# Experts sorted by load into places of 256 to 128 slots, in a two-layer hybrid diffusion step on one core

## The reference

```
def swiglu(h, w1, w3, w2):
    return (jax.nn.silu(h @ w1) * (h @ w3)) @ w2

def moe_swiglu(h, router, w1, w3, w2):
    probs = jax.nn.softmax((h @ router).astype(jnp.float32), axis=-1)
    top_p, top_i = lax.top_k(probs, TOP_K)
    top_p = top_p / jnp.sum(top_p, -1, keepdims=True)
    gates = jnp.sum(jax.nn.one_hot(top_i, N_EXPERTS, dtype=jnp.float32) * top_p[..., None], axis=-2)
    y = jnp.zeros(h.shape, jnp.float32)
    for e in range(N_EXPERTS):
        y = y + gates[..., e:e + 1] * swiglu(h, w1[e], w3[e], w2[e]).astype(jnp.float32)
    return y.astype(h.dtype)
```

## Time and profile before

| | |
|---|---|
| median of 3 runs | 2710.22 us (2710.1 to 2718.47) |
| the profiled execution | 2724.16 us, span 2722.3 us |
| mean granted TensorE clock | 0.975 |
| TensorE, VectorE, ScalarE busy | 93%, 51%, 41% |
| instructions | 68039 |

### The profile page before, as it was taken

The page is one execution under the profiler, slowest core; times in us unless marked ns, Lnnn a source line. Parts: engine busy times, 40 slices in busy tenths (PEclk is TensorE's granted clock), DMA queues, the critical chain, the costliest instruction groups (busy, mean ns, idle before and its releaser), DMA issues.

```text
span 2722.3 us, 68039 instructions
## 1 busy us (share of the span) xinstructions
PE 2521.7 (93%) x30324; PEld 2197.1 (81%) x30324; DVE 1401.3 (51%) x2474; ACT 1128.5 (41%) x2126; POOL 146.1 (5%) x163
## 2 busy tenths in 40 slices
PE   6998799898899999989987999998999999999996
PEld 3996577676798999969965777766899999999995
DVE  2337455556533333362374665474565555555565
ACT  3226544544421211242255545444444444444452
POOL 0002000010000000010010010001000000000011
PEclk8999899999999999999998999998999999999998
DMA  7223023320122222222200222202765666566672
GB/s 273 78 78 127 24 74 96 96 75 27 70 77 72 78 78 78 72 72 78 78 11 1 66 66 66 65 5 109 240 209 178 214 212 207 183 211 211 181 259 83
DMA packets 82701, 304.58 MB, mean 112 GB/s; under 512 B 9376, under 2 KB 9504, under 8 KB 82272
## 3 DMA queue, kind: packets, MB, share of 16 engines
q1 hardware_dynamic: 71072, 257.93, 29.6%
q0 software_dynamic: 11328, 42.21, 4.2%
HBM read 273.11 MB, written 27.00 MB: 110 GB/s over the span
## 4 chain that ended last, share of the span: by engine, by line
PE 83%; DVE 8%; issue 3%; ACT 3%; DMA 1%; POOL 0%; SPq 0%; another core or an unknown queue 0%; DVEq 0%; ACTq 0%; POOLq 0%
PE ps L451 19%; PE ps L452 19%; PE ps L453 19%; PE ps L1183 7%; PE ps L812 3%; PE ps L917 2%; PE ps L464 2%; PE ps L1115 2%; PE ps L960 1%; PE ps L976 1%; DMA ring<-in_blocks 1%; PE ps L463 1%; DVE arena L2474 1%; DVE arena L2473 1%; PE ps L1167 1%
## 5 line engine op out<-in xcount | busy, mean ns | idle before, releaser
L2278 DVE TENSOR_TENSOR ring_lo<-ring,w_ffn 128x1024 fp32r<-128x1024 f32 x264 | 322.5, 1225 | 214.5 <-ACT w_ffn L1702 208.5
L451 PE MATMUL ps<-hg_hi,w_ffn 128*128 128x256 f32 x1408 | 402.5, 286 | 3.2 <-DVE hg_lo L2909 3.2
L452 PE MATMUL ps<-hg_lo,w_ffn 128*128 128x256 f32 x1408 | 398.0, 283 | 0.0
L453 PE MATMUL ps<-hg_hi,ring_lo 128*128 128x256 f32 x1408 | 397.5, 282 | 0.0
L1702 ACT ACTIVATE w_ffn<-ring 128x1024 fp32r<-128x1024 f32 x264 | 278.1, 1057 | 197.7 <-PE ps L453 196.2
L451 PEld LDWEIGHTS ps<-hg_hi,w_ffn 128*128 128x128 f32 x1408 | 267.4, 190 | 4.8 <-DVE hg_lo L2909 3.4
L452 PEld LDWEIGHTS ps<-hg_lo,w_ffn 128*128 128x128 f32 x1408 | 266.5, 189 | 1.2
L453 PEld LDWEIGHTS ps<-hg_hi,ring_lo 128*128 128x128 f32 x1408 | 267.0, 190 | 0.0
L1183 PEld LDWEIGHTS ps<-arena 64*64 64x64 f32 x7680 | 165.0, 135 | 98.1 <-issue 78.5
L453 PE MATMUL ps<-hT_ffn_hi,ring_lo 128*128 128x320 f32 x704 | 216.0, 307 | 0.0
L1183 PE MATMUL ps<-arena 64*64 64x64 f32 x7680 | 190.5, 222 | 22.6 <-issue 22.2
(11 more groups left out here) (375 smaller groups left out, 5107.1 us busy)
## 6 DMA issues: line engine op xcount, KB each, us to landing
ring<-in_blocks SPq DMA_DIRECT2D x484, 512.0 KB, 3.7
h_rows<-arena POOLq DMA_DIRECT2D x16, 512.0 KB, 10.2
arena<-h_rows POOLq DMA_DIRECT2D x7, 1024.0 KB, 9.9
y_rows<-arena POOLq DMA_DIRECT2D x7, 1024.0 KB, 6.6
x<-in_x_all SPq DMA_DIRECT2D x1, 2560.0 KB, 13.2
h_plain<-arena POOLq DMA_DIRECT2D x1, 2560.0 KB, 11.6
out_y_all<-x POOLq DMA_DIRECT2D x5, 512.0 KB, 3.7
w<-in_low POOLq DMA_DIRECT2D x2, 768.0 KB, 6.4
```

Source lines behind the costliest of these rows:

```text
L451: nc.tensor.matmul(dst, w_hi, m_hi, start=start, stop=False)
L452: nc.tensor.matmul(dst, w_hi, m_lo, start=False, stop=False)
L453: return nc.tensor.matmul(dst, w_lo, m_hi, start=False, stop=stop)
L2278: V.tensor_tensor(ring_lo[:, n % RING, :], ring[:, n % RING, :], high[:, n % high.shape[1], :], ALU.subtract).then_inc(*E.sig("w_lo"))
```

## The change

The experts are sorted by the number of their tokens on chip and get places of fixed size: 256, 240, 208, 192, 176, 160, 144, 128 slots. Place 0 has the expert with the most tokens. The further passes are taken when any expert has more tokens than its place has slots.

VectorE works out the order in the routing (about 20 small instructions more, eight of them ahead of the write of the experts' numbers) and writes the eight numbers to `flag_i[1:9]`; SyncE waits for them before the first block of the first expert, loads them into eight registers, and addresses each block by the register of its place. The flag of the overflow is now loaded behind expert 0.

`up` multiplies the high weights with the high and low tokens at once (one matmul of 2n columns, side by side in one bank) and the low weights with the high tokens (n columns) into the first half. VectorE adds the two halves with a reduction over pairs (`summed`), once for w1 and once for w3, before the hidden values are formed. The banks of `up` rotate over three for each block instead of two for each round; the transposes of the next expert have one bank instead of two. Each block is now converted when the block three before it has been used. `down`, gather, transposes and output go by the tiles of a place, of which place 7 has one.

```
+RANK_CAP = [256, 240, 208, 192, 176, 160, 144, 128]
...
+        def up_bank(f, w):
+
+            return 4 + (2 * f + w) % 3
...
+        def up_at(f, w):
+
+            return 2 * f + w + max(0, f - 1)
...
+        def halves(bank, n):
+
+            return ps[:, bank, 0:2 * n].rearrange("p (h n) -> p h n", h=2)
+
+        def summed(bank, n):
+
+            return ps[:, bank, 0:2 * n].rearrange("p (h n) -> p n h", h=2)
...
             for n in range(N_BLOCKS):
+                if n == MOE_FIRST:
+                    sp.wait_ge(sem["rt_rank"], 2)
+                    expert = [sp.value_load(flag_i[0:1, 1 + p:2 + p], min_val=0, max_val=NE - 1) for p in range(NE)]
...
+                    p, c = divmod(n - MOE_FIRST, EXP_B)
+                    sp.dma_start(ring[:, n % RING, :], blocks[bass.ds(expert[p] * EXP_B + (MOE_FIRST + c), 1)].rearrange("n p d -> p (n d)")).then_inc(ring_sem[n % RING], 16)
...
             def up(k, f):
-                hi, lo = hg(k)
-                if f >= 2:
-                    pe.wait_ge(sem["eh_lo"], hidden_before(k) + f - 1)
+                m, n = hg(k), slots(k)
                 for w in range(2):
+                    if 2 * f + w >= 3:
+                        pe.wait_ge(sem["up_ev"], up_before(k, f, w) - 2)
                     w_h, w_l = split_blk(w_ffn)
+                    both = halves(up_bank(f, w), n)
                     for kc in range(KC):
                         c = slice(kc * P, (kc + 1) * P)
-                        mm = mm_split(nc, ps[:, 4 + f % 2, w * CAP:(w + 1) * CAP], w_h[:, c], w_l[:, c], hi[:, kc, :],
-                                      lo[:, kc, :], kc == 0, kc == KC - 1)
+                        nc.tensor.matmul(both, w_h[:, c], m[:, :, kc, 0:n], start=kc == 0, stop=False)
+                        mm = nc.tensor.matmul(both[:, 0, :], w_l[:, c], m[:, 0, kc, 0:n], start=False, stop=kc == KC - 1)
                     done(mm)
...
             def down(k, g):
-                for s in range(2):
-                    slots = slice(s * P, (s + 1) * P)
+                for s, rows in tiles(k):
+                    r = slice(s * P, s * P + rows)
```

On ScalarE:

```
-            def hidden(k, f):
...
-                act.wait_ge(sem["block_used"], first + up_done(f))
+            def hidden(k, f, more):
...
+                w_hi(w_ffn, first + up_at(f, 0) + 3)
+                act.wait_ge(sem["up_ev"], up_before(k, f, 0) + 1)
...
-                A(ftmp[:, f % 2, 0:CAP], ps[:, 4 + f % 2, 0:CAP], ACT.Tanh, scale=0.5).then_inc(*E.sig("eh_th"))
-                for n in ahead(f)[0]:
-                    w_hi(w_ffn, first + n)
+                A(ftmp[:, f % 2, 0:n], u_sum[:, 0:n], ACT.Tanh, scale=0.5).then_inc(*E.sig("eh_th"))
+                if more or f < FE - 1:
+                    w_hi(w_ffn, first + up_at(f, 1) + 3)
                 act.wait_ge(sem["eh_g"], hidden_before(k) + f + 1)
...
+                if f >= 1 and (more or f < FE - 1):
+                    w_hi(w_ffn, first + up_at(f, 1) + 4)
```

On VectorE, the first of the new instructions of the routing, and the hidden values:

```
+                V.scalar_tensor_tensor(key, ps[:, 1, 40:48], float(NE), C("iota")[:, 0:NE], ALU.mult, ALU.subtract).then_inc(*E.sig("dve_step"))
...
+                V.tensor_tensor(above, key.unsqueeze(1).broadcast_to([P, NE, NE]), key.unsqueeze(2).broadcast_to([P, NE, NE]), ALU.is_gt).then_inc(*E.sig("dve_step"))
...
+                V.tensor_reduce(rank, above, AX.X, ALU.add).then_inc(*E.sig("dve_step"))
...
+            def hidden(k, f, more):
...
+                t, u, v = ftmp[:, f % 2, 0:n], u_sum[:, 0:n], v_sum[:, 0:n]
+                dve.wait_ge(sem["block_used"], first + up_at(f, 0) + 1)
+                V.tensor_reduce(u, summed(up_bank(f, 0), n), AX.X, ALU.add).then_inc(*E.sig("up_ev"))
+                w_lo(w_ffn, first + up_at(f, 0) + 3)
+                dve.wait_ge(sem["block_used"], first + up_at(f, 1) + 1)
+                dve.wait_ge(sem["eh_lo"], hidden_before(k) + f)
+                V.tensor_reduce(v, summed(up_bank(f, 1), n), AX.X, ALU.add).then_inc(*E.sig("up_ev"))
                 dve.wait_ge(sem["eh_th"], hidden_before(k) + f + 1)
+                V.scalar_tensor_tensor(t, t, 1.0, u, ALU.add, ALU.mult).then_inc(*E.sig("dve_step"))
...
+                V.scalar_tensor_tensor(v, t, 0.5, v, ALU.mult, ALU.mult).then_inc(*E.sig("eh_g"))
+                if more or f < FE - 1:
+                    w_lo(w_ffn, first + up_at(f, 1) + 3)
...
+                V.tensor_tensor(ge_lo[:, f % 2, 0:n], v, ge_hi[:, f % 2, 0:n], ALU.subtract).then_inc(*E.sig("eh_lo"))
+                if f >= 1 and (more or f < FE - 1):
+                    w_lo(w_ffn, first + up_at(f, 1) + 4)
```

More of the change, by code:

```diff
@@ L366, in build @@
         yrow = take(NT * NE, i=NT, e=NE)
+        above = take(NE * NE, e=NE, q=NE)
+        place = take(NE * NE, e=NE, q=NE)
+        ptmp = take(2 * NE * NE, b=2, e=NE, q=NE)
+        key, rank, pos, cap_e, eid, over_e, y_base = (take(NE) for _ in range(7))
+        last_rk, last_gate = take(NT), take(NT)
         pick = take(2 * NT, w=2, i=NT)
@@ L2972, in moe_expert @@
                 if e < NE - 1:
[L2973 to L2974 removed]
+                    w_lo(w_ffn, first + EXP_B + 2)
                 else:
```

257 lines of the change are left out of this document (139 added, 118 removed).

## The result

The changed kernel takes 2601.98 us in the median of four runs (2594.97 to 2613.0), the kernel before 2714.34 beside it (2710.1 to 2721.21). The ratio is 0.9587, with an interval of 0.9544 to 0.9631: 4.1% faster. The forecast was 2594, in a range of 2562 to 2652. The profiled execution took 2613.0 us, with a span of 2611.2.

The account below looks back on a forecast made before the run. The eight experts were taken as bound by TensorE's matmul stream. 117 us gained there plus 3 at the end less 4 for routing made 116 us, taking the median from 2710.22 to 2594 us, range 2562 to 2652.

Parts of the forecast that it names:

- TensorE's price of an up-product: In the experts' up-products, a product costs 0.44 ns per column plus 0.006 us, with a floor of 0.114 us.
- no floor: Rival: weight loads hide wholly behind narrow up-products, places 1 to 6 gain another 27 us, 2567 us; chance 10%.
- unreduced f32 rate: Rival: the narrow up-product costs 0.84 ns per column, 52 us lost over places 1 to 6, 2646 us; chance 12%.
- The wait at each end: At each expert's end, TensorE's 1.4 us wait in the last round goes and 0.3 us per expert stays.
- VectorE and ScalarE in the rounds: New reductions stay hidden under TensorE's stream; at place 0 VectorE needs 6.9 us a round against TensorE's 8.5.
- A chain of waits: Rival: hand-overs between ScalarE and VectorE cost 0.5 us in each of 77 rounds, 39 us, 2633 us; chance 10%.
- Place 7: In the last expert VectorE sets the pace and taking results back is no longer covered: 68 us with the ends.
- VectorE 5.7 a round: In the last expert's rounds, VectorE needs 5.7 us against TensorE's 5.1 and so sets the pace.
- Supply of weights: Weight blocks needed every 2.3 us at place 6 and 1.9 at place 7, up to 275 GB/s; nothing charged.
- the forecast's own sign against it: Ring loads of weight blocks landing later than they are wanted would show the prediction wrong; no size given.
- The routing: Before the first expert, waiting for the order, register loads and later block landings cost 4 us, bounds 0 and 12.
- The end: The last combination takes one tile of slots, with fewer conversions and 512-column products: 3 us gained.

Follow-up runs that it names:

- e1_three: Changed kernel with the merged up-product split again, three products of n columns, capacities kept, output not right: 2672.16 us, ratio 0.9821 to the kernel before.
- e2_wide: Changed kernel with 256 slots in places 0 to 6 and 128 in place 7, merged products kept: 2677.77 us, ratio 0.9856 to the kernel before.
- e7_extra: Changed kernel with the first reduction of each round run twice in places 0 to 6: 2601.22 us, ratio 0.9551 to the kernel before.
- e6_noback: Changed kernel with a fill of zeros instead of weighing and adding the fetched rows in the last expert: 2597.14 us, one run.
- e5_tight: Changed kernel with capacities of 240, 208, 192, 176, 160, 144, 128, 128 slots: 2572.25 us, ratio 0.9447 to the kernel before.
- e3_static: Changed kernel with blocks loaded from constant addresses in source order, no register loads or wait for the numbers: 2600.55 us, ratio 0.9574 to the kernel before.
- e8_best: Changed kernel with capacities of 240 to 128 slots, each register loaded just before its expert, and the first weighing moved to ScalarE: 2571.80 us, ratio 0.9433.

## Why the prediction was right, point by point

**TensorE's price of an up-product**, the term that carries the sum: confirmed. Line and floor gave the price of a pair within 0.003 us at every width, and 587.7 us for places 0 to 6 before the 2 us of waits, with 587.7 measured; e1_three shows the floor by itself, and e1_three and e2_wide put 61 and 69 us on the two halves. That all eight agree as closely (657.7 and 657.5) is in part luck, as 2 us too much for those waits stand against 1.8 too little at place 7. What the forecast said would show it was wrong in form: the distances alternate 0.225 and 0.110 at place 1 and 0.178 and 0.068 at place 6, not 0.218 and 0.114 or 0.133 and 0.114. By the forecast's own test ("the second of the two distances isn't near 0.114") it would have fallen at place 6, while its sum held. The rival *no floor* would have given 0.20 for a pair at place 6, the *unreduced f32 rate* 0.25 to 0.26, which is within 0.01 of what was measured there; it is the other places and e1_three that part them: at place 1 that rival had 0.42, measured were 0.335.

**The wait at each end**, 1.4 down to 0.3: confirmed, with 0.12 to 0.13 us left of the 1.14 at 256 slots (e2_wide, and place 0 of the changed kernel) and nothing at the end of places 1 to 6. Even 0.3 was too much.

**VectorE and ScalarE in the rounds**, hidden: confirmed by e7_extra. *A chain of waits* didn't come about: in the rounds of places 0 to 6 TensorE waits twice, 0.21 and 0.45 us, for low weights.

**Place 7**: the time was 69.8 for 68, and the mechanism was half right. VectorE is the bound in the five rounds that take results back (e6_noback), which are 7.0 us long, and not in the other six. The step that was wrong is "VectorE 5.7 a round": measured from start to start it is 5.2 with the work on the next expert's tokens in it, which place 7 doesn't have, and TensorE's own 5.2 is as long. This hardly touched the forecast's time, because its sum didn't use the 5.7; it has 36.6 + 18.8 = 55.4 for eleven rounds, 5.04 each. Taking back cost about what it was given (1.99 us a piece for 2.03). Of the 1.8 us that were missing 0.7 are the late ring load.

**Supply of weights**: confirmed for places 0 to 6, where no ring load is late in any profile, even with 59.7 us for an expert (e5_tight). In place 7 the forecast's own sign against it came up: loads landed 0.9 to 1.3 us late in four profiles. It had set 275 GB/s against 411 and left out what GpSimd fetches there; the queues were at 412 (the 0.7 us above). That those fetches are what made the loads late wasn't tested. The addresses from registers are free (e3_static).

**The routing**, 4 us in bounds of 0 to 12: the number was met by luck, by errors that cancel. Eight register loads were taken as 2 us and are 4.5; the delay grows by half on its way to TensorE; the later start of the gather, 1.9 us, wasn't charged; and against these the kernel before lost 5.2 us in its gather that e3_static didn't lose. The change itself costs about 9 us here.

**The end**, 3 us: 2.1 measured.

**The level**: 2594 was forecast and 2602 came out. The kernel before, run once more beside it, had a median of 2714.3 for 2710.2, which is 4 of these 8 us; the medians then differ by 112.4 for 116. In the two profiled executions, which differ by 111.1 us, the count from the step gives 115.3, and 4.2 us are lost ahead of it, in code that is the same; whether that holds for the medians too isn't shown.

## What to carry to other kernels

In a stream where each f32 matmul loads its own 128x128 weights, one costs at least 0.11 us here, and products of 240 columns and fewer all sit on that floor; from there on only fewer weight loads help, by putting two streams behind one of them. Price a stream by the distance over a whole repeating pattern, on VectorE as on TensorE: neither one distance nor the sum of durations is its cost. Count a small effect from the last event of unchanged code, and load only the registers that the next transfer needs. And where a stage gets shorter, add up all that the queues carry in it: at one block every 2 us beside the rows fetched back they had no room left.

## What the runs showed of the hardware that was not expected

**Distances in a mixed stream.** With a wide and a narrow product in turn, the narrow one starts late (0.173 after a 256-column product that takes 0.119 in a stream of its own) and the wide one follows soon (0.060 after it). Why the pair splits so isn't shown.

**A register load on SyncE** takes 0.55 us, and loads don't overlap.

**Unchanged code isn't equally fast.** The step of the routing, ahead of which nothing differs between these kernels, lay anywhere between the two rows below, of e7_extra and of e8_best:

```profile
1869.95 0.20 DVE L2842 COPY side<-ps 128x40 f32<-128x40 f32 x1 [3.50 <-PE ps L1556]
```

```profile
1896.42 0.20 DVE L2848 COPY side<-ps 128x40 f32<-128x40 f32 x1 [3.50 <-PE ps L1558]
```

That is 26 us, 1% of the time, as much as the whole width of the interval above (0.9544 to 0.9631). The granted clock ahead of the step was 0.974 in the first and 0.963 in the second on the mean; one minus that, times the stretch, is 49.5 and 70.0 us, 20 of the 26. The changed kernel's profile has 70.0 as well and its step at 1886.71, so the clock isn't all of it, and what makes it differ isn't settled.

**A stall without a name.** ScalarE stood still for 3.90 us in the gather in the profile of before and for 3.87 in that of e8_best, with no releaser that the profile names, and in none of the others. Its cause stays open.
